# One decoder layer in fp32r on one core: seven quarter products for eight in two of three token-major column groups, in quarters two to four

## The reference, cut to what matters

```python
def mixer_sublayer(x, norm_g, w_in, sinks, rel_bias, pool_w, pool_scale, w_out):
    h = rms_norm(x, norm_g)
    z = h @ w_in
    qa, ka, va, qr, kr, vr, gr, up = jnp.split(z, SPLIT_POINTS, axis=-1)
    ya = sliding_window_attention(...)     # 6 query heads, 2 key heads, window 128, sinks, T5 bias
    yr = retention(...)                    # 6 heads of 64, chunks of 128, rotary on q and k
    yp = pool_mixer(up, pool_w, pool_scale)
    y = jnp.concatenate([ya, yr, yp], axis=-1)
    return x + y @ w_out
# x = mixer_sublayer(x, ...)
# x = x + square(relu(rms_norm(x) @ w_up)) @ w_down
# out = rms_norm(x)
```

## Time and profile before

| | us |
|---|---|
| median of 3 runs (2012.24 to 2013.15) | 2012.38 |
| the profiled execution | 2012.88 |
| its span, first to last instruction | 2011.1 |
| PE busy in the span | 1999.9 |
| DVE busy | 1403.9 |
| ACT busy | 890.0 |
| POOL busy | 183.1 |

### The profile page before, as it was taken

How to read it: one execution, slowest core, us unless ns; L and a number is a source line. 1 busy time by engine, 2 the same in 40 slices (tenths; PEclk the granted TensorE clock), 3 DMA queues, 4 the chain that set the end, 5 groups by cost and what they waited for, 6 DMA issues and landing times.

```text
span 2011.1 us, 26053 instructions
## 1 busy us (share of the span) xinstructions
PE 1999.9 (99%) x9568; PEld 1636.5 (81%) x9568; DVE 1403.9 (70%) x2044; ACT 890.0 (44%) x1490; POOL 183.1 (9%) x278
## 2 busy tenths in 40 slices
PE   9999999999999999999999999999999999999998
PEld 7778878877887788888888888888888888888886
DVE  5685578558756867777777767677666668667667
ACT  5343534444353436545545554455333334433333
POOL 2032123202320320000000000000000000000001
PEclk9999999999999999999999999999999999999999
DMA  8223412531352233576855657787947578756572
GB/s 313 75 95 133 145 63 75 194 105 64 102 195 76 95 125 100 147 184 170 171 152 136 152 143 185 175 194 198 407 183 287 196 287 335 285 195 267 196 290 84
DMA packets 102523, 350.68 MB, mean 174 GB/s; under 512 B 10331, under 2 KB 12284, under 8 KB 84988
## 3 DMA queue, kind: packets, MB, share of 16 engines
q1 hardware_dynamic: 99280, 338.22, 52.9%
q10 hardware_dynamic: 3116, 10.80, 1.5%
HBM read 271.26 MB, written 77.73 MB: 174 GB/s over the span
## 4 chain that ended last, share of the span: by engine, by line
PE 93%; DVE 2%; POOL 2%; DMA 1%; ACT 1%; issue 1%; SPq 0%; POOLq 0%; ACTq 0%; DVEq 0%
PE bank L2208 29%; PE bank L2210 29%; PE bank L2209 29%; PE bank L2309 1%; POOL qT L907 1%; PE bank L2338 1%; DMA stage<-in_wmix 1%; PE bank L2385 1%; DVE ring_lo L1730 1%; PE bank L2429 1%; PE bank L2324 1%; DVE hT_lo L1509 1%; PE bank L2388 0%; DMA xT<-in_xt 0%; PE bank L2393 0%
## 5 line engine op out<-in xcount | busy, mean ns | idle before, releaser
L2208 PE MATMUL bank<-h_hi,w_lo 128*128 128x512 f32 x912 | 355.7, 390 | 0.2 <-DVE h_lo L1714 0.2
L2210 PE MATMUL bank<-h_hi,w_hi 128*128 128x512 f32 x912 | 354.8, 389 | 0.0
L2209 PE MATMUL bank<-h_lo,w_hi 128*128 128x512 f32 x912 | 354.8, 389 | 0.0
L2208 PE MATMUL bank<-d_hi,u_lo 128*128 128x512 f32 x896 | 348.5, 389 | 0.0
L2209 PE MATMUL bank<-d_lo,u_hi 128*128 128x512 f32 x896 | 348.5, 389 | 0.0
L2210 PE MATMUL bank<-d_hi,u_hi 128*128 128x512 f32 x896 | 348.5, 389 | 0.0
L1355 ACT ACTIVATE u_hi<-u_raw 128x1024 fp32r<-128x1024 f32 x112 | 118.6, 1059 | 325.2 <-PE bank L2210 312.0
L1972 DVE TENSOR_TENSOR u_lo<-u_raw,u_hi 128x1024 fp32r<-128x1024 f32 x112 | 137.1, 1224 | 177.7 <-ACT u_hi L1355 177.7
L2208 PE MATMUL bank<-ring_hi,hT_lo 128*128 128x512 f32 x544 | 219.8, 404 | 0.0
L2210 PE MATMUL bank<-ring_hi,hT_hi 128*128 128x512 f32 x544 | 212.8, 391 | 0.0
L2209 PE MATMUL bank<-ring_lo,hT_hi 128*128 128x512 f32 x544 | 212.4, 390 | 0.0
(11 more groups left out here) (222 smaller groups left out, 3033.6 us busy)
## 6 DMA issues: line engine op xcount, KB each, us to landing
u_raw<-u_dram SPq DMA_DIRECT2D x56, 1024.0 KB, 4.8
d_raw<-in_wdn SPq DMA_DIRECT2D x56, 1024.0 KB, 6.9
stage<-in_wmix SPq DMA_DIRECT2D x100, 512.0 KB, 4.4
u_dram<-ur SPq DMA_DIRECT2D x32, 1280.0 KB, 9.7
wraw<-in_wup SPq DMA_DIRECT2D x128, 256.0 KB, 3.8
e_raw<-in_wdn SPq DMA_DIRECT2D x24, 1024.0 KB, 9.0
xq<-in_x SPq DMA_DIRECT2D x16, 512.0 KB, 3.7
x_dram<-xq ACTq DMA_DIRECT2D x16, 512.0 KB, 3.3
```

What stands on the lines that cost most here:

```text
L2208: pe.matmul(dst, al, bh, start=(first and k == 0), stop=False, skip_group_check=chain)
L2209: pe.matmul(dst, ah, bl, start=False, stop=False, skip_group_check=chain)
L2210: last = pe.matmul(dst, ah, bh, start=False, stop=(final and k == n - 1), skip_group_check=chain)
```

## The change

In quarters two to four, column groups 0 and 1 (512 tokens, K = 1024, 1024 columns) are computed as a 2 x 2 block product: tokens in two halves of 256, K in two halves of 512, columns in two halves of 512. Seven products with sums take the place of eight. Each product is 4 steps for either of two token blocks: 56 steps instead of 64, and a round has 11 steps instead of 12. The first quarter keeps the twelve tiles; `direct_in(q)` tells them apart.

What comes with it:
- **Sums of tokens** (`scaled_a21`, `a_sums`): 4 ACT and 16 DVE instructions of 128 x 256 at the start of the quarter, then 4 ACT and 4 DVE instructions of 128 x 1024 that split the sums (`s_high`, `s_low`). The high halves lie in the place of xq, so four x blocks are loaded a second time later in the quarter.
- **Sums of weights** (`quadrant_sums`): formed once, in the first quarter, by 4 x 4 DVE instructions of 128 x 512, in the places of bias0 and junk, loaded and stored by ACT's queue, into tw_dram.
- **Units**: 14 instead of 8 for the two groups, so 33 for a quarter; a unit now serves 12 matmuls, before 24.
- **Evictions**: 8 by ACT (`w_out`) and 6 by DVE (`w_add`, bank times factor plus what lies in zt); the two token blocks of a product alternate between banks 0, 1 and banks 2, 7, and a bank is taken up again 12 steps after its last one.
- **Attention**: scaling the probabilities moves from DVE to ACT (`normalize`); `att_out` of blocks 0 to 2 goes to bank 6 in place of bank 7; two copies of the bias fall away.
- The hand-written orders of both engines are new for these quarters (`dve_rounds`, `act_rounds`).

```diff
-NU = 27
+NUS = (27, 33, 33, 33)
...
+            def scaled_a21(q):
+
+                act.wait_ge(ru_done.sem, ru_done.before(q, 3))
+                act.wait_ge(gated_done.sem, gated_done.before(q, 6))
+                for c in range(4):
+                    act.activation(s_raw(0, c), xT[:, c, 256:512], ACT.Copy, scale=gcol[:, c:c + 1]).then_inc(wact_done.sem, 1)
...
+            def w_out(q, k):
+
+                j, p = divmod(k, 2)
+                act.wait_ge(tile_done.sem, tile_done.group(q, k))
+                blk, cols = {W_P1: (p, 0), W_P6: (p, 512), W_P5: (2 + p, 512), W_P4: (2 + p, 0)}[j]
+                bank_of = (dense[2], OB)[p] if j == W_P5 else dense[p]
+                act.wait_ge(rstd_done.sem, rstd_done.now(q, blk))
+                act.activation(zt[:, blk, cols:cols + 512], bank_of[:, :], ACT.Copy, scale=rstd[:, blk:blk + 1]).then_inc(wact_done.sem, 1)
+
+            def normalize(q, i):
+
+                k = i % 2
+                act.wait_ge(norm_done.sem, norm_done.now(q, 2 * i + 1))
+                for h in range(3):
+                    v = score_buf(i // 2)[:, k, 256 * h:256 * h + P]
+                    act.activation(v, v, ACT.Copy, scale=rinv[:, k, h:h + 1]).then_inc(pn_done.sem, 1)
+
+            def quadrants_load(c):
+
+                if c:
+                    act.wait_ge(s_tw, 64 * c)
...
+                act.dma_start(tsum[:, :, :], wquad[c, :, 0:1536].rearrange("p (a n) -> p a n", a=3)).then_inc(s_tw, 16)
+                act.dma_start(tsum4[:, :], wquad[c, :, 1536:2048]).then_inc(s_tw, 16)
+
+            def sums_store(c):
+
+                act.wait_ge(s_tsum, 4 * c + 4)
+                act.dma_start(tw_dram[0:3, c].rearrange("a p n -> p a n"), tsum[:, :, :]).then_inc(s_tw, 16)
+                act.dma_start(tw_dram[3, c], tsum4[:, :]).then_inc(s_tw, 16)
...
+            def act_rounds(q):
+
+                w_out(q, 0)
...
+            def w_add(q, k):
+
+                j, p = divmod(k, 2)
+                dve.wait_ge(tile_done.sem, tile_done.group(q, k))
+                blk, cols, first = {W_P2: (p, 0, W_P1), W_P7: (2 + p, 512, W_P5), W_P3: (p, 512, W_P6)}[j]
+                dve.wait_ge(wact_done.sem, wact(q, "out", 2 * first + p))
+                bank_of = dense[p] if j == W_P7 else (dense[2], OB)[p]
+                v = zt[:, blk, cols:cols + 512]
+                dve.scalar_tensor_tensor(out=v, in0=bank_of[:, :], scalar=rstd[:, blk:blk + 1], in1=v,
+                                         op0=ALU.mult, op1=ALU.add).then_inc(wdve_done.sem, 1)
+
+            def quadrant_sums(c):
+
+                dve.wait_ge(s_tw, 64 * c + 32)
...
+            def dve_rounds(q):
+
+                split_lo(q, 3)
...
+                gsteps = GSTEPS if direct_in(q) else GSTEPS - 1
                 for i in range(8):
-                    proj_G(q, GSTEPS * i, GSTEPS * i + GSTEPS // 2)
+                    proj_G(q, gsteps * i, gsteps * i + 6)
                     if i in (2, 4, 6):
                         att_out(q, i // 2 - 1)
                     if i < 6:
                         att_scores(q, i + 2)
-                    proj_G(q, GSTEPS * i + GSTEPS // 2, GSTEPS * i + GSTEPS)
+                    proj_G(q, gsteps * i + 6, gsteps * i + gsteps)
                     att_transposes(q, i)
```

More of the change, by code:

```diff
@@ L68 @@
 SCALED = (3, 5, T_UP1)
[L71 to L77, removed]
-SLOT = 3 * [0, 1, 2, 3, 4, 5] + [1, 0, 2, 3, 4, 5, 1, 2, 3]
-def slot_owner(u):
-    same = [v for v in range(min(u, NU)) if SLOT[v] == SLOT[u % NU]]
+SLOT = 3 * [0, 1, 2, 3, 4, 5] + [1, 0, 2, 3, 4, 5, 1, 2, 3]
+W_GROUPS = 14
+W_STEPS = 4 * W_GROUPS
+W_P1, W_P2, W_P6, W_P5, W_P7, W_P3, W_P4 = range(7)
@@ L88, in slot_owner, with direct_in, unit, slot @@
+W_S = {W_P5: 0, W_P6: 1, W_P7: 2, W_P3: 3}
+W_T = {W_P7: 0, W_P5: 1, W_P6: 2, W_P4: 3}
+def direct_in(q):
+    return q == 0
+def unit(q, u):
+    return u if direct_in(q) or u < 6 else u + 6
+def slot(q, u):
+    if direct_in(q):
+        return SLOT[u]
+    return u % 6 if u < 20 else SLOT[u - 6]
+def slot_owner(q, u):
+    same = [v for v in range(u) if slot(q, v) == slot(q, u)]
     if same:
[L89 to L95, removed]
+        return q, same[-1]
+    if q == 0:
+        return None
+    return q - 1, max(v for v in range(NUS[q - 1]) if slot(q - 1, v) == slot(q, u))
@@ L615, in mixer_loads @@
                     store_rows()
-                for u in range(STAGE + 2, NU if last else NU + 1):
+                for u in range(STAGE + 2, NUS[q]):
                     load_weights(q, u)
@@ new lines, in dve_rounds, with mixer_dve @@
+                rot_a(q, 2)
+                rot_add(q, 2)
+                evac_pt(q, 6)
+                softmax(q, 7)
+                gate_of(q, 0)
+                rot_a(q, 3)
+                rot_add(q, 3)
+                evac_pt(q, 7)
+                gate_of(q, 1)
+                split_lo(q, 26)
+                split_lo(q, 27)
+                pool_first(q, 0)
+                pool_rest(q, 0)
+            def mixer_dve(q, last):
+                dve.wait_ge(o_done.sem, o_done.before(q, 3))
+                dve.wait_ge(pool16_done.sem, pool16_done.before(q, 7))
+                ev, k = evac_of(T_UP1)
+                dve.wait_ge(ev.sem, ev.before(q, k))
+                dve.wait_ge(v_evac.sem, v_evac.before(q, 3))
+                dve.tensor_copy(kT[:, 0:P], kT[:, QT:QT + P]).then_inc(carried.sem, 1)
+                dve.tensor_copy(vtok[:, 0, :], vtok[:, NB, :]).then_inc(carried.sem, 1)
+                dve.tensor_copy(up[:, :, 0:PADW], up[:, :, QT:QT + PADW]).then_inc(carried.sem, 1)
+                if direct_in(q):
+                    dve_rounds_direct(q)
+                else:
+                    dve_rounds(q)
+                split_lo(q, unit(q, 22))
+                split_lo(q, unit(q, 23))
@@ L2230, in proj_T @@
             def proj_T(q, t):
-                pe.wait_ge(wlo_done.sem, wlo_done.now(q, t if t < 6 else 18))
+                pe.wait_ge(wlo_done.sem, wlo_done.now(q, t if t < 6 else unit(q, 18)))
                 free_bank(q, t)
@@ L2322, in att_transposes @@
                     pe.wait_ge(pt_evac.sem, pt_evac.now(q, 2 * i - 3))
+                    if i % 2 and not direct_in(q):
+                        pe.wait_ge(yAlo_done.sem, yAlo_done.now(q, (i - 3) // 2))
                 for h in range(3):
@@ L2328, in att_out @@
                 pe.wait_ge(pt_evac.sem, pt_evac.now(q, 4 * b + 3))
+                if b == 3 and not direct_in(q):
+                    pe.wait_ge(wdve_done.sem, wdve(q, "out", 11))
                 if b:
```

593 lines of the change are left out of this document (454 added, 139 removed).

## The result

| | before | after |
|---|---|---|
| median, us | 2012.4 (7 runs, 2012.1 to 2013.2) | 2019.9 (7 runs, 2016.8 to 2022.0) |
| span of the profiled execution, us | 2011.1 | 2018.1 |
| PE busy, us | 1999.9 | 1990.7 |
| PE not busy, us | 11.2 | 27.4 |

The ratio is 1.0037, with a 95% interval of 1.0025 to 1.0048: the change makes the kernel slower by 7.5 us, where I had forecast 3.1 us off and a range that ends at 2016.5. Two things in the table already say where to look. PE has 16.2 us more in which it does nothing. And it works 9.2 us less, where 72 matmuls at 0.2267 us should have taken 16.3 away: some 7 us of work are back. The runs also scatter over 5.2 us, where those of before scatter over 1.0.

A forecast was written before the change was run, and what follows sets the result against it. PE was taken to bound the kernel, so any added PE wait adds time. From the profiled 2012.9: -16.3 matmuls, +11.1 `att_out` waits, +2.1 first quarter gave 2009.8, 2009.3 us at the median; range 1998.0 to 2016.5.

The forecast's parts named there:

- 72 matmuls fewer: Quarters two to four: groups go from 96 steps to 88, at 0.2267 us a matmul, -16.3 us.
- `att_out` of round 6, three quarters: PE waits some 3.7 us for `evac_pt(5)` in each of quarters two to four, 11.1 us in three.
- first quarter: Four sets of weight sums on DVE make PE wait: 1.4 us at masked scores plus 0.7, together 2.1 us.
- What bounds the kernel: Whole kernel: PE, busy 1999.9 of 2011.1 us; any wait an edit adds to PE is added to the time.
- The rounds: Quarters two to four: DVE waits 10.1 us for ACT in rounds 2 to 5, so `evac_pt(5)` ends at 486.4.
- the last rival: PE's clock falls behind the three `att_out` stalls: 6 us lower level each, 9 us more, 2018.3 us; chance 0.15.
- The second set: First quarter: two sets of weight sums, 2.7 us each, fall into rounds with that much idle time on DVE.
- The 0.7 us for the fourth set's load: First quarter: ACT's load of the fourth set waits for stores to land ahead of the pooled rows, 0.7 us.
- hold the pace: Rival in the rounds: some DVE waits are shorter and no PE wait is left there, 1998.2 us; chance 0.2.
- Weights were not late in the rounds: Rival: if landing takes 7 us, units 15 and 23 are late, 5.6 us wait a quarter, 2015.0 us; chance 0.1.
- The tail of the quarter is as before: After round 7 DVE is in step with PE again, so no new wait follows in the quarter.
- Token sums at nothing: Sums at the quarter's start cost nothing under some 5 us of cover, up to 1 us a quarter if thinner.

The follow-up runs named there:

- first_quarter: The changed kernel with only the first quarter's weight sums further back, the rounds of quarters two to four unchanged: 2013.65 us.
- ends_ahead: The changed kernel with reordered rounds, first-quarter sums and last high half further back, then the first quarter's second set of sums moved ahead on DVE: 2006.58 us.
- the last version: The 2006.58 us version with the first block's masked retention scores ahead of a low half and an output tile's sum on DVE, quarters two to four: 2004.56 us.

## Why the prediction was wrong

| term, us | forecast | profiled execution |
|---|---|---|
| 72 matmuls fewer | -16.3 | -16.3 (-15.3 by the busy time of `first_quarter`, 1984.6) |
| `att_out` of round 6, three quarters | +11.1 | +9.1 |
| first quarter | +2.1 | +5.6 (3.7 and 1.9) |
| other waits | 0 | +1.5 |
| lower clock behind the waits | 0 | +6.8 to 7.1 |
| sum | -3.1 | +7.0 |

- **What bounds the kernel**: right. Each us of new idle time of PE is in the time, and the matmul's price held to 1 us in 16.
- **The rounds**: right in place, mechanism and nearly in size. DVE waited for a high half as laid out: 2.57, 2.00, 2.00, 0.96 and 2.18 us in the third quarter against 2.6, 2.0, 2.0, 1.1 and 2.4. Three of these rows:

```profile
452.29 1.23 DVE L1989 TENSOR_TENSOR ring_lo<-stage,ring_hi 128x1024 fp32r<-128x1024 f32 x1 [2.57 <-ACT ring_hi L1098]
...
460.82 1.23 DVE L1989 TENSOR_TENSOR ring_lo<-stage,ring_hi 128x1024 fp32r<-128x1024 f32 x1 [2.00 <-ACT ring_hi L1098]
...
486.39 2.36 DVE L1989 TENSOR_TENSOR ring_lo<-stage,ring_hi 128x1024 fp32r<-128x1024 f32 x2 [2.18 <-ACT ring_hi L1098]
```

  From `evac_pt(1)` (448.42) to the end of `evac_pt(5)` (491.5) it is 43.1 us; the forecast's 443.2 to 486.4 is 43.2. The wait was 3.0 instead of 3.7 since PE came to `att_out` 40.2 us behind `evac_pt(1)` (488.6), where the forecast has 39.6 (482.8).
- **The clock, the step that failed.** The sum set the lower clock at nothing; it stood only as the last rival, at 0.15, because no row that was read shows PE at the lower level. That was no evidence against it: between its first and last matmul PE had never stood for more than 1.1 us, so rows from there could not have shown it. And one place of the trace of before does speak: PE's last matmul ends at 2003.04, and these windows follow.

```profile
2003.00:2004.00 1.00, 0.04 (x1) 0.00 (x0) 0.92 (x2) 0.20 (x1) 0.64 (x2) 1.00 0.32 127
...
2005.00:2006.00 1.00, 0.00 (x0) 0.00 (x0) 1.00 (x2) 0.36 (x2) 0.77 (x2) 0.86 0.04 12
2006.00:2007.00 1.00, 0.00 (x0) 0.00 (x0) 0.36 (x1) 0.00 (x0) 0.92 (x2) 0.50 0.00 0
```

  The granted clock was at half by 2006, some 3 us after PE stopped, with DVE and POOL still at work. The forecast put waits of 3.7 us in three places, and said that the trace neither bears out nor speaks against a lower clock behind them; these rows speak for it. The rival's mechanism happened, its size was over: 9 us forecast, some 7 measured, of which 1.7 belong to the first quarter and 5.1 to two of the three stalls at `att_out`. With this case as the likeliest the forecast would have been 2018.3.
- **The first quarter, mis-sized.** The place (masked scores) was right. A set of sums took 5.2 us and not 2.7, because its price came from an operation that POOL doesn't slow, and POOL's own rows at that time weren't looked at. The second set, said to fit into idle time, made PE wait 1.9 us. It took 5.0 us too (100.56 to 105.59), beside POOL, and its store stood ahead of two high halves on ACT. The store's place was the smaller part: with the store moved the wait was 1.5 us, and with the set itself moved on DVE as well (`ends_ahead`) 0.3. The 0.7 us for the fourth set's load did not come: between 150 and 300 us PE's waits are 0.3 us, before 0.2. With the clock at nothing and this term right, the forecast would have been 2012.8, still in the range; the clock put the result outside it.
- **The rivals.** The rounds did not hold the pace. Weights were not late in the rounds; at their end one load was, hidden behind the wait at `att_out` until the order was mended (2.2 us a quarter). "The tail of the quarter is as before" held only as long as PE came late to it.
- **Token sums at nothing**: no wait of PE at the start of a quarter, as said.

Not tried: the price of ACT's scaling apart from its place in the order, and the waits that the last version still has (4.9 us in four ahead of the retention scores, for which the profile names no releaser, and 2.8 us in five for zt). Why the same wait is followed by the lower level in one execution and not in the next stays open.

## What to carry to other kernels

Where PE is always busy, price a new wait at its length and, once it is longer than any that the trace shows at full clock, at the work lost behind it as well: 1.6 us each here for waits of 3.3 us, and a chance of as much from 1.4 us on. A trace without long waits says nothing against that; look at what the clock does once PE has stopped at its end. And before taking an instruction's length from a row, look at what ran beside it, on DVE at POOL above all; when one wait goes, look for the next in line, which it may have hidden.

## What the hardware showed that I had not expected

- Whether the clock falls is not fixed by the program. The same waits of 3.0 us were followed by 1.00 or less from quarter to quarter, and the time of one program differs from run to run: 7 us between the fastest and the slowest of eleven runs (0.999 and 0.995).
- Work that nobody needs can pay: 39 matmuls, 8.8 us of PE's time, took 3.05 us off.
- The lower level lasts on when the wait is over: in the third quarter it covered `att_out` itself, 2.83 us for 8 matmuls instead of 1.51, and the group matmuls behind it.
- DVE's sums of two SBUF tensors took twice their length beside POOL, 1.43 to 1.64 us instead of 0.68.
